# Adding expert rows to token rows in DRAM: indirect accumulating transfers in place of selection products in the first layer

## The reference, cut to what matters

```python
gates, idx = lax.top_k(affinity, cap)
xs = jax.vmap(lambda hb, ib: hb[ib])(h, idx)
a = jnp.einsum('becd,edf->becf', xs, w_gate)
u = jnp.einsum('becd,edf->becf', xs, w_up)
y = jnp.einsum('becf,efd->becd', jax.nn.silu(a) * u, w_down) * gates[..., None].astype(h.dtype)
return jax.vmap(lambda yb, ib: jnp.zeros((n, d), yb.dtype).at[ib.reshape(-1)].add(yb.reshape(-1, d)))(y, idx)
```

## Time and profile before

| what | us |
|---|---|
| median of 3 runs | 2274.07 |
| lowest and highest | 2272.76, 2274.79 |
| the profiled execution's own time | 2275.11 |
| its span, first to last instruction | 2273.3 |
| PE busy | 2070.3 (91%) |
| DVE busy | 812.8 (36%) |
| ACT busy | 503.2 (22%) |
| POOL busy | 123.6 (5%) |
| mean granted clock of PE | 0.966 |

### The profile page before, as it was taken

The page is one execution under the profiler, slowest core; times in us unless marked ns, Lnnn a source line. Parts: engine busy times, 40 slices in busy tenths (PEclk is TensorE's granted clock), DMA queues, the critical chain, the costliest instruction groups (busy, mean ns, idle before and its releaser), DMA issues. The chain is left out here.

```text
span 2273.3 us, 27399 instructions
## 1 busy us (share of the span) xinstructions
PE 2070.3 (91%) x10742; PEld 980.8 (43%) x10742; DVE 812.8 (36%) x2106; ACT 503.2 (22%) x1176; POOL 123.6 (5%) x130
## 2 busy tenths in 40 slices
PE   5999989999988999999999799999999699898886
PEld 3445455556633333333333456455565233333332
DVE  3323256778650111130211531377766301010102
ACT  3211244545431010000100321154444100000000
POOL 1101000000001000000000110000000000000000
PEclk9999988999988999999999999999999799999999
DMA  8841200000089988889879202020003899999995
GB/s 334 303 147 53 52 23 1 1 1 1 19 331 426 394 355 349 355 332 398 337 323 371 97 19 74 1 75 1 1 1 148 356 426 427 427 426 427 426 427 214
DMA packets 87690, 504.67 MB, mean 222 GB/s; under 512 B 10162, under 2 KB 15196, under 8 KB 33292
## 3 DMA queue, kind: packets, MB, share of 16 engines
q1 hardware_dynamic: 82912, 487.00, 53.2%
q0 software_dynamic: 2880, 10.49, 1.2%
q10 hardware_dynamic: 1772, 5.43, 0.6%
HBM read 495.55 MB, written 7.34 MB: 221 GB/s over the span
## 5 line engine op out<-in xcount | busy, mean ns | idle before, releaser
L598 PE MATMUL psS<-arena 128*64 128x512 f32 (+9 forms) x4544 | 1165.5, 558 | 52.1 <-DMA arena<-in_w_up 18.0
L598 PEld LDWEIGHTS psS<-arena 128*64 128x64 f32 (+4 forms) x4544 | 460.0, 159 | 651.4 <-issue 590.1
L601 PE MATMUL psT<-ident,arena 128*128 128x128 f32 (+2 forms) x936 | 154.0, 294 | 68.2 <-DVE arena L1752 23.9
L1899 DVE TENSOR_TENSOR arena<-arena,psS 128x512 f32<-128x512 f32 x32 | 20.6, 685 | 496.2 <-PE psS L598 496.2
L1101 ACT ACTIVATE arena<-psS 128x128 f32<-128x128 f32 (+5 forms) x150 | 57.3, 412 | 592.5 <-PE psS L598 529.7
L598 PE MATMUL psO<-arena 128*64 128x128 f32 (+2 forms) x1664 | 182.4, 310 | 1.5 <-issue 1.5
L601 PEld LDWEIGHTS psT<-ident,arena 128*128 128x128 f32 (+2 forms) x936 | 110.8, 147 | 155.7 <-issue 98.3
L1101 ACT ACTIVATE arena<-psS,nb 128x768 f32<-128x768 f32 (+2 forms) x200 | 159.1, 795 | 78.6 <-DVE nb L1743 77.3
L598 PE MATMUL psT<-arena 128*32 128x512 f32 x1536 | 174.7, 595 | 0.0
L1738 DVE TENSOR_REDUCE mx<-psS 128x1 f32<-128x768 f32 (+2 forms) x200 | 165.0, 825 | 19.6 <-PE psS L598 17.9
L598 PE MATMUL psM<-arena 128*128 128x512 f32 x352 | 157.7, 595 | 0.5 <-ACT arena L1101 0.5
(11 more groups left out here) (217 smaller groups left out, 1378.3 us busy)
## 6 DMA issues: line engine op xcount, KB each, us to landing
arena<-in_w_gate SPq DMA_DIRECT2D x116, 1024.0 KB, 12.3
arena<-in_w_up SPq DMA_DIRECT2D x116, 1024.0 KB, 12.0
arena<-in_w_down SPq DMA_DIRECT2D x116, 1024.0 KB, 12.2
arena<-in_w_mod SPq DMA_DIRECT2D x40, 1024.0 KB, 9.1
arena<-in_w_in SPq DMA_DIRECT2D x6, 2048.0 KB, 7.8
gtb<-in_w_mod SPq DMA_DIRECT2D x8, 1024.0 KB, 6.5
normed_rows<-arena ACTq DMA_DIRECT2D x10, 512.0 KB, 13.8
arena<-in_w_out SPq DMA_DIRECT2D x8, 512.0 KB, 7.8
```

Source lines behind the costliest of these rows:

```text
L598: return nc.tensor.matmul(o, lhsT, rhs, start=start, stop=stop)
L601: return nc.tensor.transpose(o, in_, ident[0:n, 0:n])
L1899: last = V.tensor_tensor(ar[:, a:a + 512], ar[:, a:a + 512], bank(2 * g + h), ALU.mult)
```

## The change

In the first layer the rows of quads 0, 1 and 2 are no longer combined by products. SP stores X (3 MB) in a DRAM tensor `sums` before the chunk loads of stage 6 of quad 0. For each of these quads POOL issues eight indirect transfers that add rows to `sums` (4 of 64 latent rows, 4 of 32 context rows, each row 4 KB). Each waits for the transfer before it of its kind. They stand on POOL ahead of the gathers of quad q + 2, or at the end. SP loads X back from `sums` before the chunk loads of stage 6 of quad 3. The Silu of quad q + 1 waits for the adds of quad q in place of `ce`. Only quad 3 has `selection`, the split and `combine`.

In the second layer all four quads are combined by products as before, but split and in fp32r (32 products in place of 16 plain ones). In both layers the last quad's jobs go round six banks instead of two. The transposes of the next quad's tokens end one stage earlier (TURN_AT_2). At the end of the kernel the final gains are loaded before the sums, and the root and the scaled rows are done in two pairs of tiles. Some semaphores are shared between the layers.

```diff
+COMBINED = ((NQ - 1,), tuple(range(NQ)))
-TURN_AT_2 = {(8, 0): (0,), (8, 1): (1,), (9, 0): (2,), (9, 1): (3,), (10, 0): (4,), (10, 1): (5,), (11, 0): (6,), (11, 1): (7,)}
+TURN_AT_2 = {(8, 0): (0,), (8, 1): (1,), (9, 0): (2, 3), (9, 1): (4,), (10, 0): (5,), (10, 1): (6, 7)}
+SUMS_STORED_AT, SUMS_LOADED_AT = 6, (NQ - 1) * NSTAGE + 6
...
+        COMBINE_BANKS = ((6, 7), (6, 7, 0, 1, 2, 3))
...
@@ SP, loop over chunks
+                    if l == 0 and n == SUMS_STORED_AT * QUAD:
+                        sp.wait_ge(z["xr"], TT)
+                        sp.dma_start(sums.rearrange("(t p) d -> p t d", p=P), X[:, :].rearrange("p (t d) -> p t d", t=TT)).then_inc(s_sum, 16)
+                    if l == 0 and n == SUMS_LOADED_AT * QUAD:
+                        sp.wait_ge(s_addl, 16 * QUAD * (NQ - 1))
+                        sp.wait_ge(s_addc, 16 * QUAD * (NQ - 1))
+                        load(X[:, :].rearrange("p (t d) -> p t d", t=TT), sums.rearrange("(t p) d -> p t d", p=P), s_sum)
...
-            sp.wait_ge(Z[L - 1]["ffn_done"], L)
+            sp.wait_ge(Z[L - 1]["fgev"], 4 * L)
             load(gfin, A["g_final"].partition_broadcast(P), s_x)
@@ POOL
+                def added(q):
+                    if q == 0:
+                        pool.wait_ge(s_sum, 16)
+                        pool.wait_ge(z["lgev"], 1)
+                    for e in range(QUAD):
+                        g, p0 = e // 2, e % 2 * CAP_L
+                        pool.wait_ge(z["y"], hidden_tile(l, q, g))
+                        if q or e:
+                            pool.wait_ge(s_addl, 16 * (QUAD * q + e))
+                        nc.gpsimd.indirect_dma_start(
+                            out=sums, out_offset=bass.IndirectOffsetOnAxis(ap=idx[0:CAP_L, q * QUAD + e:q * QUAD + e + 1], axis=0),
+                            in_=ar[p0:p0 + CAP_L, F["HID"] + g * D:F["HID"] + (g + 1) * D], in_offset=None,
+                            bounds_check=NTOK - 1, compute_op=ALU.add).then_inc(s_addl, 16)
+                    for e in range(QUAD):
+                        p0, c = e * CAP_C, NE + q * QUAD + e
+                        pool.wait_ge(z["y"], hidden_tile(l, q, 2))
+                        if q or e:
+                            pool.wait_ge(s_addc, 16 * (QUAD * q + e))
+                        nc.gpsimd.indirect_dma_start(
...
+                            bounds_check=NTOK - 1, compute_op=ALU.add).then_inc(s_addc, 16)
...
-                    elif q == 1:
-                        pool.wait_ge(z["gp"], KD)
+                    elif q == 1 or l == 0:
+                        if q > 1:
+                            added(q - 2)
+                        pool.wait_ge(z["gp"], KD * q)
...
+                if l == 0:
+                    added(NQ - 2)
@@ PE
-                        if st == 0 and q:
+                        if st == 0 and q - 1 in COMBINED[l]:
                             combine(q - 1)
@@ ACT, before the Silu
-                        if q:
+                        if q and wc:
+                            act.wait_ge(s_addl, 16 * QUAD * q)
+                            act.wait_ge(s_addc, 16 * QUAD * q)
+                        elif q:
                             act.wait_ge(z["ce"], q * NC)
@@ DVE
+                            V.tensor_scalar(idx[0:CAP_L, 0:NE], bank(4, 0, CAP_L, 0, NE), float(CTX), None, ALU.add)
+                            link(V.tensor_copy(idx[0:CAP_C, NE:2 * NE], bank(4, 0, CAP_C, 32, NE)))
...
                 for q in range(NQ):
-                    if q:
+                    if q - 1 in COMBINED[l]:
                         combined(q - 1)
-                    selection(q)
+                    if q in COMBINED[l]:
+                        selection(q)
...
+                if l < L - 1:
+                    dve.wait_ge(s_sum, 32)
+                    combined(NQ - 1)
...
             dve.wait_ge(s_x, 16 * (L + 1))
+            combined(NQ - 1, range(6))
+            final_root(0)
+            combined(NQ - 1, range(6, 8))
+            rsqrt_end(2)
+            final_rows(0)
+            final_rows(1)
+            final_root(1)
+            rsqrt_end(2)
+            final_rows(2)
+            final_rows(3)
```

More of the change, by code:

```diff
@@ L372, in backbone_program @@
         Z = [sems(l, "sq xn ht htev htevd proj pact pdve dsq bsq bt btev bs bsa bsd kn kpe kt "
-                     "S nb P mixed T PTa PTd O Og mj me gp ge cp ce xg") for l in range(L)]
-        once = {n: sem(n) for n in "open want gd gt gtev rbp rb fg fgev yh yl wb wo lgev pe_ex prb at dup dupT ffn_done xready fxn_sq fxn xr lp st xt xtd lgp lgpc xp done silu prod hp Cn bn qs he y win0 win1".split()}
+                     "S nb P T PTa PTd O mj me gp ge cp ce") for l in range(L)]
+        once = {n: sem(n) for n in "open want gd gt gtev rbp rb fg fgev yh yl wb wo lgev pe_ex prb at dup dupT ffn_done xready fxn_sq fxn xr lp st xt xtd lgp lgpc xp done silu prod hp Cn bn qs he y win0 win1 mixed Og xg".split()}
         for z in Z:
@@ L404, in hidden_tile, with combine_index, split_tile @@
             return l * NQ * (SW[0] // P) + q * (SW[l] // P) + g + 1
+        def combine_index(l, q):
+            return COMBINED[l].index(q)
+        def split_tile(l, q, g):
+            return l * len(COMBINED[0]) * (SW[0] // P) + combine_index(l, q) * (SW[l] // P) + g + 1
         block = ctx.enter_context(nc.Block())
@@ L411, in backbone_program, with rounded, combine_bank @@
         rows = nc.dram_tensor("normed_rows", (NTOK, D), f32).ap()
+        sums = nc.dram_tensor("summed_rows", (NTOK, D), f32).ap()
         FP = [places(l) for l in range(L)]
[L415 to L418, removed]
+        def rounded(name, cols, at):
+            return nc.alloc_sbuf_tensor_at(name, [P, cols], f32r, offset=arena_at + 4 * at)
+        assert FP[0]["STL"] == FP[1]["STL"]
+        stl_r = rounded("selection_r", 2 * LAT + CTX, FP[0]["STL"])
+        YHR = [rounded(f"output_high{l}", SW[l] // P * D, FP[l]["YH"]) for l in range(L)]
+        YLR = [rounded(f"output_low{l}", SW[l] // P * D, FP[l]["YL"]) for l in range(L)]
+        COMBINE_BANKS = ((6, 7), (6, 7, 0, 1, 2, 3))
+        def combine_bank(q, n):
+            banks = COMBINE_BANKS[q == NQ - 1]
+            return banks[n % len(banks)]
+        gfin = modrow[:, 2048:2048 + D]
         @block.sync
@@ L989, in _ @@
                 turns = TURN_AT if wc else TURN_AT_2
-                free = {6: None, 7: None}
+                yh_r, yl_r = YHR[l], YLR[l]
+                free = {b: None for b in range(8)}
                 def take(b):
@@ L1025, in combine @@
                             a = 2 * LAT + t * P if g == 2 else g * LAT + (t - TC) * P
[L1026 to L1031, removed]
-                                last = mm(bank(b), ar[:, a:a + P], ar[:, r:r + 512], g == groups[0], g == groups[-1])
+                            mm(bank(b), stl_r[:, a:a + P], view(yh_r, 0, P, 4 * h * W + g * P, (W, 4), (1, P)), g == groups[0], False)
+                            r = g * D + h * 512
+                            last = mm(bank(b), stl_r[:, a:a + P], yl_r[:, r:r + 512], False, g == groups[-1])
                         last.then_inc(z["cp"], 1)
-                        free[b] = (z["ce"], q * len(CJ) + n + 1)
+                        free[b] = (z["ce"], c * len(CJ) + n + 1)
                 def group(q, st, g):
@@ L1378, in _ @@
                         modulated(x, 6 + x % 2)
-                    for g in range(NX if wc else 0):
+                    for g in range(NX if q in COMBINED[l] else 0):
                         act.wait_ge(z["y"], hidden_tile(l, q, g))
@@ L1391, in _ @@
                     c = t if l < L - 1 else n
-                    j = VV if l < L - 1 else F["HIDT"]
-                    a_(ar[:, j:j + D], X[:, t * D:(t + 1) * D], ACT.Square,
+                    a_(ar[:, VV:VV + D], X[:, t * D:(t + 1) * D], ACT.Square,
                        accum_out=ss[:, c:c + 1]).then_inc(done, 1)
```

82 lines of the change are left out of this document (44 added, 38 removed).

## The result

| | before | after |
|---|---|---|
| median of 5 runs each, us | 2274.07 (2272.38 to 2280.10) | 2289.09 (2285.95 to 2289.96) |
| profiled execution, us (span) | 2275.11 (2273.3) | 2287.81 (2286.0) |
| granted clock, mean over the span | 0.966 | 0.953 |

The kernel became slower: the ratio is 1.0054, 95% interval 1.0041 to 1.0067. I had predicted 2260 us. The time lies in the range given (2236 to 2294), but the direction is wrong.

The account below looks back on a forecast made before the run. PE's work was taken to bound the first layer's experts, the weight stream the second's. Terms -33.0 + 21.6 - 0.7 - 2.5 = -14.6 us gave 2260 us, range 2236 to 2294.

Parts of the forecast that it names:

- The products are worth 33.0 us: First layer's quad boundaries: dropping the combining products of three quads takes 11.00 us each off PE's path.
- The chain is 53.9 us: POOL's eight adds of a first-layer quad: seven links in sequence, 256 KB adds landing in 7.3 us, 128 KB in 6.0.
- the room of 46.7: Time in us from a quad's first weighted rows until its adds must be done for the next quad's Silu and stage 4.
- second read of 0.6: Each 256 KB add also reads its destination row at the stream's 427 GB/s, 0.6 us more than a copy.
- A stall of 7.2 us, three times 21.6: PE waits before stage 4 of quads 1, 2 and 3 while the chain overruns: 21.6 us in all (0 to 41.7).
- The upper end by bytes: Chain of adds if destination reads cost a gather's pace: 60.6 us, 13.9 over the room, stalls of 42 us.
- Rival 4: Silu after stage 3: chain over 58.8 us makes the kernel slower, a second trip of 2.5 us per link; 2294 us, chance 0.23.
- Rival 1: First layer's adds are hidden, with no stall: gain of 36.2 us, 2238 us (2235 to 2246), chance 0.25.
- X's transfers hidden, the ring keeps its lead: First layer: X's store and load, 7.4 us of stream each, cost nothing; SP is held 7.2 us, like PE.
- DMA to 0.93: Sign in the first layer's profile after: DMA share rises to 0.93 or so, from 0.89.
- End of the first layer -0.7: Last quad's twelve jobs: with six banks, DVE's last add comes about 0.7 us earlier (0 to 1.5).
- End of the kernel -2.5: After the second layer's last weighting: products 1.9 us sooner, root and scaling 0.6 sooner, together 2.5 us.

Follow-up runs that it names:

- plain write: Changed kernel with its 24 adding transfers overwriting their rows instead of adding, so the first layer's sums are lost: 2273.5 us in one run.
- the kept-busy kernel: Changed kernel with 14 products of unread result put before PE's wait for the Silu at stage 4 of quads 1 to 3: 2281.37 us, ratio 1.0018.
- the order in turn: Changed kernel with the same eight adds of a quad issued as latent and context adds alternately: 2244.67 us, ratio 0.9848.
- the gather buffer: Changed kernel with weighted rows of quads 0 to 2 written there, so the next gathers, not the Silu, wait for adds; X loaded three stages later: 2240.04 us.
- the three kernels without stalls: Changed kernel with first-layer products put back (2270.89 us), with latent and context adds alternating (2244.67), or with weighted rows in the gather buffer (2240.04).

## Why the prediction was wrong

- *The products are worth 33.0 us*: right. A quad without them and without a stall takes 135.43 us, 11.01 less.
- *The chain is 53.9 us*: the step that failed first, by the size of its links. It is 59.65, 60.26 and 57.67 us in the three quads. The form was right (seven links, the Silu, PE's stage 4, the room of 46.7), the size was not. In quad 0 a latent link was put at 8.07 us and is 9.10, the pair at 9.38 and is 10.29, a context link at 6.77 and is 7.33; with the two ends 5.75 us too little. Over the nine latent links of the three quads an add's link is 8.86 us on average, a plain write's 8.14, and my copy's was 7.42. So nearly all of the 0.79 us is that a copy of rows to DRAM behind the stream costs 0.72 more than I had read from the gathers. For the addition I gave 0.65 and it takes 0.73, but not as I thought: 0.48 of it is POOL's longer issue, and what is left, 0.25, does not bear out my second read of 0.6. The release took 0.8 to 0.9 us where I gave 0.77. These are averages over one execution of each kernel, with links from 8.13 to 9.60 and from 7.60 to 8.89. One landing, 8.8 us, lies outside the 5.2 to 8.5 that I had named as a sign of being wrong.
- *A stall of 7.2 us, three times 21.6*: 12.90, 13.50 and 10.91, together 37.3. The forecast chain is longer than the room by a seventh only, so some 10% more on the chain made the stall 1.7 times as long. This alone moves the forecast of -14.6 to +1.1.
- *A missing term*: nothing in the sum stood for the granted clock behind the stall. It cost 2.6, 1.9 and 2.8 us, and in the kept-busy kernel those groups take 7.09 again. With it a quad loses 14.9 us on average for 11.0 gained, and the sum is +8.4.
- *The upper end by bytes* (60.6 us, 13.9 over) was 1 us from the truth, but not for its reason. The Trainium skill (Collectives: The Full Stack, section The bandwidth ceiling) measures a collective's reduce step, an add in a DMA engine, at half the rate of a copy for large sizes. That rule, taken over to these small adds, would have made the better forecast of this chain. No run shows the rule at work: adds and writes differ by 4.7 us of 58.3 on average, more than half of it in POOL's issue.
- *Rival 4* named the place, the direction and the point: the chain is over 58.8 us (59.2 on average), and the stall, 12.4 on average, just over the 12.1 that breaks even. It fails as a mechanism. Its second trip of 2.5 us a link would be 17.5 us; all that the addition costs is 4.7 (6.8 at most). And stalls just past that point are worth about +1 us; what made the kernel clearly slower is the clock, 7.3 us behind the stalls and 4.8 in the second layer, which the threshold left out. So the chance given to slower was right for a reason that did not hold.
- *Rival 1* (hidden) is what the order in turn and the gather buffer bring about. Its 2238 us stands beside 2244.67 and 2240.04 measured, on a chip where the kernel before took 4 us more.
- *X's transfers hidden, the ring keeps its lead*: right. SP waited 9.3 us for the adds (I had put 7.2), and PE waited for no weight.
- *DMA to 0.93*: it stayed at 0.89 to 0.90, since stalls lengthened the quads. Without stalls it is 0.99, more than my at most 129 us of 135.4, and the two kernels near it show the first waits for weights, 1.5 us and 4.2 us in all, 2.5 of these behind the load of X. So X's transfers are hidden beside the stalls, and not quite where there are none.
- *End of the first layer -0.7*: -0.1. In the three kernels without stalls the same stretch takes 11.4 to 11.6 us for 12.68 before, so the six banks are worth 1.1 to 1.3; in the changed kernel the lower clock takes that back. *End of the kernel -2.5*: -3.0. The first product comes 4.02 us behind the weighting (2260.85 to 2264.87), as taken, and from the last add's start to the end of scaling it is 8.84 us (8.8 taken); the products are 2.3 us sooner for 1.9:
```profile
2260.85 1.41 DVE L1977 SCALAR_TENSOR_TENSOR arena<-psS,LG,gtb 128x512 f32<-128x512 f32 x2 [0.97 <-PE psS L657]
...
2274.04 0.69 DVE L1955 TENSOR_TENSOR X<-X,psM 128x512 f32<-128x512 f32 x1 [0.21 <-PE psM L657]
```
- *A second term that was missing*: 4.8 us at the start of the second layer, where the granted clock is lower after than before. All five executions with a stall in the last quad have 2 to 5 us of it. How a stall in the first layer comes to lower the clock there stays open. With it, the two ends and the first stretch the sum comes to the +12.7 between the profiled executions, within 0.3.

## What to carry to other kernels

Before work is moved from a busy engine to transfers that wait for one another, ask whose buffer they hold, and set the number of links times one link, with its issue and release, under the load of that stage, against the time until the buffer is wanted. Where the two are within a fifth of each other, interleave independent chains or read from a buffer that nobody wants soon; here the one was worth 44 us and the other 49, without taking a byte of the adds away. A stall of PE costs more than its length: here 37.3 us of stalls brought 7.3 us of slower work right behind them, and with them went 2 to 5 us later on. Making such a stall shorter does not make that price smaller until it is nearly gone: behind 6.05 us it was still 2.8, behind 2.91 and 2.42 it was nothing.

## What the runs showed of the hardware that I had not expected

- An indirect add of 64 rows took POOL 1.40 us to issue (32 rows: 1.31), the same transfer as a write 0.92 and 0.87.
- Behind a stream that fills the DMA engines, a small indirect transfer pays some 3 us (latent link 9.1 us, 5.7 without the stream), most of which does not go with its size.
- PE idle for 6.05 to 15.85 us was followed by 32 matmuls in 8.6 to 10.0 us in place of 7.09, at a granted clock of 0.73 where it was looked at; behind 2.42 and 2.91 us they took 7.09. Kernels with such idle times also had 0.66 in place of 0.83 in a pause of PE 90 us and more later, and those with one in the last quad took 2 to 5 us more to the first gather of the next layer.
